# Reordering the first projection, the last state-space step and two norms of a four-layer diffusion backbone

## What is computed

```python
hx = modulate(rmsnorm(x, norm1_w[i]), mod_x[:, 0], mod_x[:, 1])   # h * (1 + scale) + shift
x  = x + mod_x[:, 2][:, None] * mixer(hx)      # block 0: state space, block 1: attention
hx = modulate(rmsnorm(x, norm2_w[i]), mod_x[:, 3], mod_x[:, 4])
x  = x + mod_x[:, 5][:, None] * channel(hx)    # block 0: dense SwiGLU, block 1: top 2 of 8 experts
```

```python
dt = softplus(dt_raw + dt_bias);  acum = cumsum(dt * a)      # per chunk and head
y_intra = (C B^T * exp(acum_i - acum_j) * dt_j) x            # inside a chunk
y_state = C state * exp(acum)                                # carried from chunk to chunk
out = gated_rmsnorm(y + d_skip * x, z, norm_w) @ w_out
```

## Time and profile before

| | us |
|---|---|
| median of 3 runs | 2229.24 (2227.0 to 2232.21) |
| the profiled execution | 2228.91 |
| its span, first to last instruction | 2227.1 |
| PE busy | 2112.6 (95%) |
| DVE busy | 1487.7 (67%) |
| ACT busy | 1208.3 (54%) |

### The profile page before, as it was taken

How to read it: one execution, slowest core, us unless ns; L and a number is a source line. 1 busy time by engine, 2 the same in 40 slices (tenths; PEclk the granted TensorE clock), 3 DMA queues, 4 the chain that set the end, 5 groups by cost and what they waited for, 6 DMA issues and landing times.

```text
span 2227.1 us, 26875 instructions
## 1 busy us (share of the span) xinstructions
PE 2112.6 (95%) x11268; PEld 1706.9 (77%) x11268; DVE 1487.7 (67%) x1421; ACT 1208.3 (54%) x1256; POOL 62.7 (3%) x20
## 2 busy tenths in 40 slices
PE   6899999989899999989878999999999999999997
PEld 4678888767677777868567888888888888888885
DVE  3578888753333232235646888898888988888885
ACT  4566665632322222224646767676767666676763
POOL 0111111100000000000000000000000000000000
PEclk9999999989899999999988999999999999999998
DMA  7233454522244544322215999899998989999891
GB/s 310 90 140 133 173 199 157 191 76 76 90 175 152 180 160 157 113 99 97 114 60 215 365 339 353 340 360 355 343 355 343 353 338 351 343 368 347 344 353 54
DMA packets 71776, 510.08 MB, mean 229 GB/s; under 512 B 7968, under 2 KB 8352, under 8 KB 10976
## 3 DMA queue, kind: packets, MB, share of 16 engines
q1 hardware_dynamic: 71568, 508.15, 60.3%
q10 hardware_dynamic: 80, 0.13, 0.0%
HBM read 504.97 MB, written 3.28 MB: 228 GB/s over the span
## 4 chain that ended last, share of the span: by engine, by line
PE 82%; DVE 10%; ACT 4%; issue 2%; DMA 1%; SPq 0%; POOL 0%; POOLq 0%; DVEq 0%; ACTq 0%
PE ps L1086 14%; PE ps L1084 14%; PE ps L1085 14%; PE ps L659 10%; PE ps L661 10%; PE ps L660 10%; PE ps L778 1%; DVE area L1804 1%; PE ps L1068 1%; PE ps L1115 1%; PE ps L671 1%; DVE d_lo L1675 1%; DVE area L1855 1%; DVE area L1832 1%; PE ps L1145 1%
## 5 line engine op out<-in xcount | busy, mean ns | idle before, releaser
L2137 DVE TENSOR_TENSOR w_lo<-w_raw,w_hi 128x2048 fp32r<-128x2048 f32 x336 | 748.5, 2287 | 59.0 <-ACT w_hi L1551 59.0
L1551 ACT ACTIVATE w_hi<-w_raw 128x2048 fp32r<-128x2048 f32 x336 | 625.3, 1919 | 77.2 <-PE ps L1086 76.0
L1675 DVE TENSOR_TENSOR d_lo<-d_raw,d_hi 128x2048 fp32r<-128x2048 f32 (+1 forms) x76 | 171.9, 2262 | 317.2 <-ACT d_hi L1255 317.2
L1084 PE MATMUL ps<-w_hi,x_hi 128*128 128x512 f32 x896 | 358.5, 400 | 5.1 <-DVE x_lo L2192 5.1
L1086 PE MATMUL ps<-w_hi,x_lo 128*128 128x512 f32 x896 | 356.3, 398 | 0.0
L1085 PE MATMUL ps<-w_lo,x_hi 128*128 128x512 f32 x896 | 351.9, 393 | 0.0
L659 PE MATMUL ps<-h_top,d_hi 128*128 128x512 f32 (+1 forms) x816 | 329.1, 403 | 19.3 <-DVE h_low L1667 9.5
L1255 ACT ACTIVATE d_hi<-d_raw 128x2048 fp32r<-128x2048 f32 (+1 forms) x76 | 143.8, 1892 | 365.6 <-DMA d_raw<-in_dense 228.2
L661 PE MATMUL ps<-h_top,d_lo 128*128 128x512 f32 (+1 forms) x816 | 320.7, 393 | 0.0
L660 PE MATMUL ps<-h_low,d_hi 128*128 128x512 f32 (+1 forms) x816 | 316.9, 388 | 0.0
L659 PEld LDWEIGHTS ps<-h_top,d_hi 128*128 128x128 f32 x816 | 156.7, 192 | 62.3 <-issue 24.5
(11 more groups left out here) (291 smaller groups left out, 2504.5 us busy)
## 6 DMA issues: line engine op xcount, KB each, us to landing
w_raw<-in_experts SPq DMA_DIRECT2D x336, 1024.0 KB, 4.8
d_raw<-in_dense SPq DMA_DIRECT2D x120, 1024.0 KB, 5.2
area<-acum_rows SPq DMA_DIRECT2D x16, 1024.0 KB, 7.3
d_raw<-in_dense SPq DMA_DIRECT2D x4, 768.0 KB, 4.3
xT<-in_xt SPq DMA_DIRECT2D x4, 512.0 KB, 6.9
gate_rows<-area SPq DMA_DIRECT2D x4, 512.0 KB, 6.7
hT<-gate_rows SPq DMA_DIRECT2D x2, 1024.0 KB, 6.1
cst<-in_consts SPq DMA_DIRECT2D x2, 512.0 KB, 12.9
```

The costliest lines, as they stand in the source:

```text
L1084: mm(o, hi, w_hi[u % HIGH][:, a:a + 512], start=first, stop=False)
L1551: A(w_hi[n % HIGH][:], w_raw[n % RAW][:], ACT.Copy).then_inc(S["whi_done"], 1)
L1675: TT(d_lo[u][:, 0:w], d_raw[u][:, 0:w], d_hi[si % D_HIGH][:, 0:w].bitcast(F32), ALU.subtract)\
L2137: TT(w_lo[n % RAW][:], w_raw[n % RAW][:], w_hi[n % HIGH][:].bitcast(F32), ALU.subtract)\
```

## The change

PE's order of the first part: pair 1, a quarter, turn 1, pairs 2 and 3, turn 2, a quarter, turn 3, half of dt, two quarters, the other half of dt. Four tiles of z come ahead of the transposes of dt, and z is cut in 4, 2, 2 tiles around them and the cumulative sums. ScalarE and VectorE follow that order, and the splits of the second to fourth unit move out of the dt and cumulative chains. ScalarE writes the rows ahead of the tail's Exp.

In the last step `gate_high(1)`/`gate_low(1)` move forward, `state_ops` goes ahead of `carried` and `decayed`, and turn 11 comes after the outputs; PE waits for `st_op` 80 in its old place. At norms 1 and 2 the weight split moves behind: on ScalarE into the tile loop, on VectorE after it.

```diff
-            for p in range(4):
-                mod_pair(p, 5 + p % 2)
-                turn_pair(p, 3 + p % 2)
-                if p == 0:
-                    norm_spread(0)
-                else:
-                    gemm_part("x", 0, (0, 1), (2 * p - 2, 2 * p - 1))
+            mod_pair(0, 5)
+            turn_pair(0, 3)
+            norm_spread(0)
+            mod_pair(1, 6)
+            gemm_part("x", 0, (0, 1), (0, 1))
+            turn_pair(1, 4)
+            mod_pair(2, 5)
+            mod_pair(3, 6)
+            turn_pair(2, 3)
+            gemm_part("x", 0, (0, 1), (2, 3))
+            turn_pair(3, 4)
+            dt_part(range(4))
+            gemm_part("x", 0, (0, 1), (4, 5))
             gemm_part("x", 0, (0, 1), (6, 7)).then_inc(S["d_used"], 1)
-            pe.wait_ge(S["wdt_lo"], 1)
-            pe.wait_ge(S["mrow_sb"], 4)
...
+            dt_part(range(4, KT)).then_inc(S["dt_ps"], 1)
             pe.wait_ge(S["gemm_evac"], 2)
             gemm_part("bc", 0, (0, 1), range(KT)).then_inc(S["d_used"], 1)
+            pe.wait_ge(S["mod_done"], 4)
+            gemm_part("z", 0, (2, 3), range(4))
             pe.wait_ge(S["dt_dve"], 1)
...
             last.then_inc(S["dt_tr"], 1)
-            pe.wait_ge(S["mod_done"], 4)
-            gemm_part("z", 0, (2, 3), range(4))
+            gemm_part("z", 0, (2, 3), (4, 5))
             pe.wait_ge(S["dt_tok"], 1)
...
-            gemm_part("z", 0, (2, 3), range(4, KT)).then_inc(S["d_used"], 1)
+            gemm_part("z", 0, (2, 3), (6, 7)).then_inc(S["d_used"], 1)
...
             mod_pair(11, 5)
-            turn_pair(11, 5)
+            pe.wait_ge(S["st_op"], 80)
             out_part(1, 0, range(8)).then_inc(S["d_used"], 1)
             outputs(7)
+            turn_pair(11, 5)
             out_part(0, 1, range(8, 14))
...
@@ ScalarE
-            def split_tiles(j, l, shift):
+            def split_tiles(j, l, shift, si):
...
+                    if k == 3:
+                        dense_high(si)
...
             one_tile = shifted(0, 0, 0, "n_id")
+            dense_high(0)
             for p in range(4):
...
                 if p == 0:
-                    dense_high(0)
-                if p == 1:
                     act.wait_ge(S["wdt_in"], 16)
...
             evac_raw(0, 1)
+            dense_high(2)
             act.wait_ge(S["dt_v"], 1)
...
-            dense_high(2)
             tap(0, 0)
             tap(0, 1)
+            evac_raw(0, 2)
+            evac_raw(0, 3)
+            dense_high(3)
             act.wait_ge(S["dt_tr"], 1)
...
-            act.wait_ge(S["ac_tail"], 1)
-            A(tail, tail, ACT.Exp).then_inc(S["ac_exp"], 1)
             act.wait_ge(S["ac_rows"], 1)
...
             act.dma_start(scr, dts[2][0:64, :]).then_inc(S["scr_out"], 16)
+            act.wait_ge(S["ac_tail"], 1)
+            A(tail, tail, ACT.Exp).then_inc(S["ac_exp"], 1)
...
             gate_high(0)
+            gate_high(1)
             segments_back(7)
             segments_forth(7)
             token_evac(7)
-            gate_high(1)
+            dense_high(W0 + 1)
             row_exps(7)
-            dense_high(W0 + 1)
...
-            dense_high(W0 + 9)
             root(1)
-            split_tiles(1, 0, 3)
+            split_tiles(1, 0, 3, W0 + 9)
...
-            dense_high(W0 + 43)
             root(2)
-            split_tiles(2, 1, 0)
+            split_tiles(2, 1, 0, W0 + 43)
@@ VectorE
-            for k in range(KT):
+            def first_mul(k):
...
-            for p in range(1, 4):
-                mod_rows(p)
-                first_low(2 * p - 2)
-                first_low(2 * p - 1)
-                if p == 1:
-                    dense_low(0)
-                mod_out(p)
-                first_alpha(p)
+            first_mul(0)
+            first_mul(1)
+            dense_low(0)
+            first_low(0)
+            first_low(1)
+            mod_rows(1)
+            for k in range(2, KT):
+                first_mul(k)
+            mod_out(1)
+            first_alpha(1)
             dv.wait_ge(S["wdt_hi"], 1)
             TT(wdt_lo[:], wdt, wdt_hi[:].bitcast(F32), ALU.subtract).then_inc(S["wdt_lo"], 1)
-            first_low(6)
-            first_low(7)
+            mod_rows(2)
+            first_low(2)
+            first_low(3)
+            mod_rows(3)
+            mod_out(2)
+            first_alpha(2)
+            mod_out(3)
+            first_alpha(3)
+            for k in range(4, KT):
+                first_low(k)
             dense_low(1)
...
             TS(v, ps[6][0:64, :], dtb, None, ALU.add).then_inc(S["dt_v"], 1)
+            dense_low(2)
...
-            dense_low(2)
             dv.wait_ge(S["dcol_op"], 3)
             convolve(0, 0)
+            dense_low(3)
...
-            dense_low(3)
             dv.wait_ge(S["ac_exp"], 2)
...
             segments(7)
+            gate_low(1)
             token_scales(7)
             merge(7)
-            gate_low(1)
+            dense_low(W0 + 1)
+            state_ops(7)
             carried(7)
             decayed(7)
-            dense_low(W0 + 1)
-            state_ops(7)
             skip(7)
             mod_rows(11)
-            mod_out(11)
             gate_low(2)
             dense_low(W0 + 2)
             gated(7)
+            mod_out(11)
             gate_low(3)
...
+            norm_split(1)
             dense_low(W0 + 9)
-            norm_split(1)
...
+            norm_split(2)
             dense_low(W0 + 43)
-            norm_split(2)
```

More of the change, by code:

```diff
@@ L785, in _, with dt_part @@
             norm_sum(0)
-            for p in range(4):
-                mod_pair(p, 5 + p % 2)
-                turn_pair(p, 3 + p % 2)
-                if p == 0:
-                    norm_spread(0)
-                else:
-                    gemm_part("x", 0, (0, 1), (2 * p - 2, 2 * p - 1))
-            gemm_part("x", 0, (0, 1), (6, 7)).then_inc(S["d_used"], 1)
-            pe.wait_ge(S["wdt_lo"], 1)
-            pe.wait_ge(S["mrow_sb"], 4)
-            for k in range(KT):
-                c = slice(P * k, P * k + P)
-                last = thrice(ps[6][:], (wdt_hi[:, c], wdt_lo[:, c]), (h_top[:, k, :], h_low_[:, k, :]), k == 0, k == KT - 1)
-            last.then_inc(S["dt_ps"], 1)
+            def dt_part(ks):
+                pe.wait_ge(S["wdt_lo"], 1)
+                for k in ks:
+                    c = slice(P * k, P * k + P)
+                    last = thrice(ps[6][:], (wdt_hi[:, c], wdt_lo[:, c]), (h_top[:, k, :], h_low_[:, k, :]), k == 0, k == KT - 1)
+                return last
+            mod_pair(0, 5)
[11 more added lines that the diff above has]
+            gemm_part("x", 0, (0, 1), (4, 5))
+            gemm_part("x", 0, (0, 1), (6, 7)).then_inc(S["d_used"], 1)
+            dt_part(range(4, KT)).then_inc(S["dt_ps"], 1)
             pe.wait_ge(S["gemm_evac"], 2)
             gemm_part("bc", 0, (0, 1), range(KT)).then_inc(S["d_used"], 1)
+            pe.wait_ge(S["mod_done"], 4)
+            gemm_part("z", 0, (2, 3), range(4))
             pe.wait_ge(S["dt_dve"], 1)
@@ L1384, in _ @@
             A(atk, ps[7][:, 256:512], ACT.Copy).then_inc(S["dt_tok"], 1)
-            evac_raw(0, 2)
-            evac_raw(0, 3)
             tap(0, 2)
             tap(0, 3)
-            dense_high(3)
             act.wait_ge(S["ac_ps"], 1)
```

## The result

The changed kernel takes 2204.03 us (median of 4 runs, 2202.54 to 2205.48), the kernel before 2230.38 beside it: ratio 0.9884, 95% interval 0.9871 to 0.9896. Forecast were 2205.6 and a range of 2199 to 2216. The profiled executions have spans of 2202.5 and 2227.1 us, 24.6 apart; the medians are 26.3 apart.

The account below looks back on a forecast made before the run. PE was taken as busy nearly throughout from group 1 on, so only its waits before and between were cut: 9.7 + 11.8 + 2.5 - 0.4 = 23.6 us, giving 2205.6 against the median 2229.24, range 2199 to 2216.

Parts of the forecast that it names:

- First part: 10.4 less 0.7: Start to line 833: reordered projections and rows write let PE resume 10.4 us earlier, less 0.7 for the clock: 9.7.
- The 0.7 for a longer low stretch: Line 833: PE's wait grows from 2.7 to 6.4 us, so the 1.2 GHz stretch after it lengthens, charged 0.7 us.
- Last step: 11.8: Last state-space step: outputs end 11.8 us earlier, with `gate_low(1)` moved forward and a 2.1 us wait for states added.
- the low stretch behind the wait of 2.14 us: Last step, behind the added `st_op` 80 wait: may bring one stretch at 1.2 GHz, 1.7 us, given only as bound.
- Norm 1: 2.5: Norm 1: reciprocal 3.0 us earlier with the weight split moved behind; gain 2.5 us, bounds 1.7 to 3.0.
- Norm 2: -0.4: Norm 2: reciprocal 2.4 us earlier, but `dense_low(W0+43)` is late for q's second block; loss 0.4 us, bounds 0 to 2.0.
- Rival 1: Rows' path or last step: one large gain is swallowed at the next join, 2217 to 2219 us; chance 0.13.
- Rival 2: Clock: waits of 6.4 and 2.1 us and norm 2's each bring a low stretch, 5 us back, 2210.5; chance 0.10.
- Rivals 3 and 4: TensorE stays at 1.2 GHz after the 6.4 us wait, 2252, chance 0.03; nothing moves, 2229, chance 0.02.

Follow-up runs that it names:

- Number 10: The changed kernel once more, nothing edited: 2201.63 us.
- 2: Kernel before with only z's tiles around transposes and cumulative sums, weight splits out of the dt chain, rows written ahead of the tail's Exp: 2220.67 us, ratio 0.9968.
- Number 3: Kernel before with the change of the last state-space step alone: 2217.13 us, ratio 0.9954.
- number 4: Kernel before with the weight split moved behind norm 1 alone: 2225.48 us, ratio 0.9987.
- number 6: Changed kernel with the last step's chunk states between tiles 5 and 6 of the first output block and state_ops ahead of merge: 2201.82 us, ratio 0.9880.
- Number 5: Changed kernel with norm 2 as before, weight split ahead of root and reciprocal: 2201.01 us, ratio to the kernel before 0.9874.
- 8: Changed kernel with norm 2 as before, earlier states in the last step, and group 0's read-out first, all together: 2202.91 us, ratio 0.9884.
- 9: Changed kernel with norm 2 as before, earlier last-step states, group 0's read-out first, and the first projection's unit loaded ahead of modulation pair 1: 2203.60 us, ratio 0.9882.
- 1: Kernel before with the quarters between the modulation pairs alone, up to the dt projection: 2224.0 us, ratio 0.9979.
- number 7: Changed kernel with, in group 0 alone, the read-out ahead of the backward exps and the states behind all eight bc tiles: 2203.16 us, ratio 0.9887.
- 11: The kernel before once more, nothing edited: 2228.56 us.

## Why the prediction was right

**First part: 10.4 less 0.7.** The steps came in the forecast order and a little early: the projection at 31.2 (31.23), dt done at 57.5 (57.30), the transposes at 74.4 (73.94), the write at 83.4 (82.40), PE back at 102.7 (101.82). The microsecond is made up of dt's 0.2, of 0.3 in bc and z, and of the transposes: 0.7 us, where I had taken the 1.1 that they took behind a wait. The 0.7 for a longer low stretch after the longer wait was wrong in this execution: 24 products took 7.45 us there, 7.38 before. Number 10 shows the case that I had priced, 8.52 us. The shift wasn't even either: from the outputs of group 0 to those of group 6 it fell from 11.2 to 10.5. A group takes 47.8 us or, with a wait of PE for VectorE at line 725, 48.6; of six, three were long in the changed kernel (1.6 us of waits in all) and two in the kernel before (1.1). That isn't the edit's: in the changed kernel's second execution none was long, in numbers 2 to 4 none either. What makes a group long is open.

**Last step: 11.8.** It measured 10.0. The term that failed is the one that I put at zero and only mentioned as a bound: the low stretch behind the wait of 2.14 us. "The wait of 2.1 us may bring one low stretch (1.7)": it brought 1.55. With it the sum is 10.2. Number 3 has the 12.1 without it, number 6 the step with a wait of 0.8 and no low stretch. The order of the rest was as forecast: states at 452.49, `g_lo` ahead of the token copies.

**Norm 1: 2.5.** 2.7 here, 3.3 in number 4. The reciprocal came 3.1 earlier relative to the sums, and TensorE, at half clock, was behind the supply when the split stood in ScalarE's way.

**Norm 2: -0.4.** -0.8: inside this stretch the mechanism is right (the wait for `d_lo`, 1.12 here and 0.9 in three more executions), and I had its size at half. Number 5 took it back and found 0.8.

**What was not in the sum.** Attention gained 1.8 with no edit in it, at a mean clock of 0.93 instead of 0.90, and that made the span's difference 24.6 where the steps give 22.8. It goes with the move at norm 2. The four executions with the move have attention at 161.7 to 162.1 us, the nine without it at 163.3 to 163.9 and, once (number 5), 166.6. Norm 2 and attention together take 192.5 to 192.7 us with the move and 193.3 to 193.9 (196.7) without. So the move that I booked as a loss of 0.4 lost 0.5 to 0.8 in its own stretch and went with a gain of more than that behind it, and taking it back (numbers 5, 8, 9) gave up the second to save the first. PE's waits in attention are the same to within a microsecond; what differs is the level (mean clock 0.92 to 0.93 with the move, 0.89 to 0.90 without). Why the move should do that is not shown.

**How much of it is luck.** Against the forecast the first part gained 1.1 more, the last step 1.8 less, norm 1 0.2 more, norm 2 lost 0.4 more, and attention added 1.8 that wasn't forecast. These nearly cancel. That the time lies in the range follows from the mechanism; that 2204.03 lies 1.6 from 2205.6 doesn't. The second pair of executions is 27.1 apart.

**The rivals.** Rival 1 (a gain swallowed at the next join) is refuted by numbers 1 to 3, each of which got its part. Its times were added up wrong: 23.6 less 9.7 or 11.8 leaves 13.9 or 11.8, so 2215.3 or 2217.4, not 2217 to 2219, and the lower one lay inside the range. Rival 2 (the clock) is half right: the wait of 2.14 us brought a low stretch, the one of 6.7 didn't make the old one longer (in number 10 it did, by 1.1). The Trainium skill ("TensorE: Matmul & The Clock Gate", Part 1) has the low level as the default, which activity releases. PE's restart behind 6.7 us (24 products in 7.45 us, where half of number 3's 48 take 5.7) agrees. Behind the short wait the level was low in four executions (12.99) and not in number 3 (11.44), so the wait alone didn't settle the level. Rivals 3 and 4 had nothing for them.

## What to carry to other kernels

Where in-order queues meet, read for each wait what stands ahead of the waited-for instruction on its engine, and move work that isn't needed yet behind it: splits, read-outs and an Exp moved off a serial chain gave 7.5 us here, and the pairs run together 2 us and more (4.4 in medians). A move into a loop is free only if the consumer is slower than the loop: behind norm 1 it was, behind norm 2, with half as many columns, it wasn't. Sum a change from stretches cut at the same instructions, and look at the unedited stretches too, over several executions: one of them moved with an edit here, against the edit's own stretch. Differences below about 3 us in 2200 were not told apart by the medians of four runs.

## What was unexpected of the hardware

An equal wait of 2.14 to 2.15 us was followed by 48 products in 12.99 us in four executions (the changed kernel twice, numbers 5 and 7) and in 11.44 us in one (number 3). The attention stretch, the same code in all, took 161.7 to 166.6 us over thirteen profiled executions of eleven kernels, at a mean granted clock of 0.93 to 0.89, and its two lengths, below 162.2 and above 163.2, go with an edit in the norm ahead of it. Taking out a wait can cost its gain again where it leaves two shorter ones (number 7: 6.5 us for outputs that take 4.85 at full clock). The same code from the start to the last step took 437.5 to 441.6 us in four executions (before, numbers 3, 4 and 11).
